# Two iterations of a feed-forward loop brought to the 512-column matmul form of the other eight, on one core

## What is computed

```python
x = x + 0.5 * swiglu(rms_norm(x, ffn1_norm), ffn1_wg, ffn1_wu, ffn1_wd)

def swiglu(x, wg, wu, wd):
    return (silu(x @ wg) * (x @ wu)) @ wd      # wg, wu: 1024 x 2816, wd: 2816 x 1024
```

## Time and profile before

| what | value |
|---|---|
| median of three runs | 859.6 us |
| the profiled execution, its own time | 859.85 us |
| its span, first to last instruction | 858.0 us |
| TensorE busy | 850.4 us (99%) |
| VectorE busy | 640.9 us (75%) |
| ScalarE busy | 526.1 us (61%) |
| granted TensorE clock, mean | 1.000 |
| 24 to 32 us: DMA share | 1.06 |

### The profile page before, as it was taken

How to read it: one execution, slowest core, us unless ns; L and a number is a source line. 1 busy time by engine, 2 the same in 40 slices (tenths; PEclk the granted TensorE clock), 3 DMA queues, 4 the chain that set the end, 5 groups by cost and what they waited for, 6 DMA issues and landing times.

```text
span 858.0 us, 12036 instructions
## 1 busy us (share of the span) xinstructions
PE 850.4 (99%) x4791; PEld 739.4 (86%) x4791; DVE 640.9 (75%) x797; ACT 526.1 (61%) x740; POOL 61.3 (7%) x68
## 2 busy tenths in 40 slices
PE   9999999999999999999999999999999999999997
PEld 8988888888889888888888888888888898888885
DVE  5999999987698756764565468759777777767773
ACT  6777777766574544653553457548766665576762
POOL 0022322210000000000000000100000001000001
PEclk9999999999999999999999999999999999999999
DMA  8976566554644655576456545686656655853501
GB/s 272 325 263 197 179 195 197 196 157 160 200 147 147 198 196 173 175 241 220 149 184 229 176 153 191 215 268 216 227 178 217 216 168 172 260 180 104 180 1 50
DMA packets 124039, 162.47 MB, mean 189 GB/s; under 512 B 3912, under 2 KB 110928, under 8 KB 123984
## 3 DMA queue, kind: packets, MB, share of 16 engines
q1 hardware_dynamic: 122176, 154.89, 55.0%
q0 software_dynamic: 1504, 6.29, 2.3%
q10 hardware_dynamic: 304, 0.53, 0.2%
HBM read 160.65 MB, written 1.05 MB: 188 GB/s over the span
## 4 chain that ended last, share of the span: by engine, by line
PE 99%; POOL 0%; DVE 0%; issue 0%; POOLq 0%
PE pAcc L452 24%; PE pG L396 9%; PE pU L396 9%; PE pAcc L396 7%; PE pG L399 5%; PE pR L396 5%; PE pU L399 5%; PE pM L396 4%; PE pAcc L399 3%; PE pR L399 2%; PE pAcc L430 2%; PE pAcc L432 2%; PE pAcc L431 2%; PE pM L399 2%; PE pG L515 1%; PE pM L430 1%
## 5 line engine op out<-in xcount | busy, mean ns | idle before, releaser
L330 DVE TENSOR_TENSOR lo<-raw,hi 128x2048 fp32r<-128x2048 f32 x131 | 298.4, 2288 | 52.3 <-ACT hi L325 52.3
L325 ACT ACTIVATE hi<-raw 128x2048 fp32r<-128x2048 f32 x140 | 265.6, 1907 | 18.2 <-PE pAcc L432 5.8
L396 PE MATMUL pG<-xT,hi 128*128 128x512 f32 x336 | 83.7, 391 | 0.0
L396 PE MATMUL pU<-xT,hi 128*128 128x512 f32 x320 | 80.2, 392 | 0.0
L452 PE MATMUL pAcc<-hi,h_hi 128*128 128x512 f32 x240 | 74.8, 393 | 0.0
L452 PE MATMUL pAcc<-lo,h_hi 128*128 128x512 f32 x240 | 74.2, 390 | 0.0
L452 PE MATMUL pAcc<-hi,h_lo 128*128 128x512 f32 x240 | 74.0, 389 | 0.0
L396 PEld LDWEIGHTS pG<-xT,hi 128*128 128x128 f32 x336 | 62.1, 188 | 13.0 <-issue 0.7
L1141 ACT ACTIVATE h_hi<-h 128x512 fp32r<-128x512 f32 x28 | 17.7, 633 | 81.0 <-PE pAcc L452 75.2
L396 PEld LDWEIGHTS pU<-xT,hi 128*128 128x128 f32 x320 | 57.5, 189 | 10.3
L1666 DVE TENSOR_TENSOR h_lo<-h,h_hi 128x512 fp32r<-128x512 f32 x28 | 19.2, 688 | 46.1 <-ACT h_hi L1141 46.1
(11 more groups left out here) (520 smaller groups left out, 1650.2 us busy)
## 6 DMA issues: line engine op xcount, KB each, us to landing
raw<-in_a_w_in SPq DMA_DIRECT2D x24, 1024.0 KB, 5.3
raw<-in_ffn_wd SPq DMA_DIRECT2D x22, 1024.0 KB, 5.6
raw<-in_ffn_wg SPq DMA_DIRECT2D x21, 1024.0 KB, 5.4
raw<-in_ffn_wu SPq DMA_DIRECT2D x21, 1024.0 KB, 6.5
raw<-in_w_in SPq DMA_DIRECT2D x16, 1024.0 KB, 5.5
raw<-in_a_w_out SPq DMA_DIRECT2D x8, 1024.0 KB, 4.9
raw<-in_w_kv SPq DMA_DIRECT2D x8, 1024.0 KB, 5.4
raw<-in_b_w_qz SPq DMA_DIRECT2D x8, 1024.0 KB, 5.4
```

The source lines that it names most:

```text
L325: act.activation(HI[n % NHL][:, :], RAW[n % NRAW][:, :], ACT.Copy).then_inc(S["hi"], 1)
L330: dve.tensor_tensor(LO[n % NHL][:, :], RAW[n % NRAW][:, :], HI[n % NHL][:, :].bitcast(f32), ALU.subtract).then_inc(S["lo"], 1)
L396: pe.matmul(v3(bank[:, :], 2), wh[:, k, w], x4[:, :, k, :], start=(k == 0), stop=False, skip_group_check=True)
```

## The change

Iterations 1 and 10 take the 512-column form too. Gate 1 goes to banks R and ACC[0] (`GATE_1`), up 1 and up 10 to G and U. The order on ScalarE and VectorE is rewritten: in iteration 1 `bias_prepare` moves behind the lo part of block 5, and H and both bias sums follow behind it; in iteration 10 `bias_out` comes behind the copies of up 10. TensorE gets a wait for the second sum of the gate in front of each contraction. The rest of the removed lines are the old branches of the same functions.

```diff
-WIDE1 = range(2, 10)
-WIDE = [("ffn1", k, i) for i in WIDE1 for k in ("gate", "up")] + [("ffn1", "gate", NF - 1)]
+WIDE1 = range(1, 10)
+WIDE = [("ffn1", k, i) for i in WIDE1 for k in ("gate", "up")] + [("ffn1", k, NF - 1) for k in ("gate", "up")]
...
         def wide_iteration(pe, i):
             gate, up = ("ffn1", "gate", i), ("ffn1", "up", i)
+            if i == 1:
+                wide_to_features(pe, gate, GATE_1, [(S["xt_lo"], 4)] * 2)
+                pe.wait_ge(S["h_first"], 1)
+                pe.wait_ge(S["h"], 1)
+                for r in range(2):
+                    for t in range(NT):
+                        end = pe.transpose(M[:, r * TOK + t * P:r * TOK + (t + 1) * P],
+                                           H[:, t * BC + r * P:t * BC + (r + 1) * P], IDENT[:, :])
+                end.then_inc(S["hT"], 1)
+                free = [(S["silu"], 1), (S["h"], 1)]
             else:
+                wide_to_features(pe, gate, (G, U), [summed(("ffn1", "up", i - 1), f) for f in range(2)])
+                free = [summed(gate, f) for f in range(2)]
             pe.wait_ge(S["lo"], NTH[up] + 1)
+            wide_to_features(pe, up, (G, U), free)
+            pe.wait_ge(*summed(gate, 1))
+            if i < NF - 1:
+                contract(pe, "ffn1", i - 1)
+        GATE_1 = (R, ACC[0])
...
         def wide_iteration_act(act, i):
...
-            hi(act, n + LEAD)
+            if i > 1:
+                hi(act, n + LEAD)
             act.wait_ge(S["h"], i)
+            banks = GATE_1 if i == 1 else (G, U)
+            wide_act(act, gate, banks, SA, 0)
+            if i > 1:
+                bias_sign(act, step_at(i, 0))
+            wide_act(act, gate, banks, SA, 1)
+            if i == 1:
+                h_hi(act, "ffn1", 0)
+                hi(act, n + LEAD)
             hi(act, n + 1 + LEAD)
             act.wait_ge(*summed(gate, 1))
             act.activation(SA[:, :], SA[:, :], ACT.Silu).then_inc(S["silu"], 1)
             wide_act(act, up, (G, U), SB, 0)
-            bias_sign(act, step_at(i, 1))
+            if i > 1:
+                bias_sign(act, step_at(i, 1))
             wide_act(act, up, (G, U), SB, 1)
+            if i == 1:
+                bias_sign(act, step_at(i, 0))
+                bias_sign(act, step_at(i, 1))
+            if i < NF - 1:
+                hi(act, n + 2 + LEAD)
+                bias_sign(act, step_at(i, 2))
+                bias_sign(act, step_at(i, 3))
+                h_hi(act, "ffn1", i)
...
         def act_ffn(act, ph):
...
+            for i in range(1, NF):
+                wide_iteration_act(act, i)
+            bias_out(act)
+            h_hi(act, ph, NF - 1)
...
         def wide_iteration_dve(dve, i):
...
+            if i == 1:
+                wide_dve(dve, gate, GATE_1, SA, 0)
+                wide_dve(dve, gate, GATE_1, SA, 1)
+                h_lo(dve, "ffn1", 0)
+                lo(dve, n + LEAD)
+                bias_prepare(dve)
+                wide_dve(dve, up, (G, U), SB, 0)
+                wide_dve(dve, up, (G, U), SB, 1)
+            else:
...
             dve.wait_ge(S["hl"], i)
             dve.wait_ge(S["silu"], i + 1)
             dve.wait_ge(*summed(up, 1))
             dve.tensor_tensor(H[:, :], SB[:, :], SA[:, :], ALU.mult).then_inc(S["h"], 1)
-            lo(dve, n + 2 + LEAD)
-            bias_sum(dve, step_at(i, 2))
-            bias_sum(dve, step_at(i, 3))
+            if i == 1:
+                lo(dve, n + 1 + LEAD)
+                bias_sum(dve, step_at(i, 0))
+                bias_sum(dve, step_at(i, 1))
+            if i < NF - 1:
+                lo(dve, n + 2 + LEAD)
+                bias_sum(dve, step_at(i, 2))
+                bias_sum(dve, step_at(i, 3))
             h_lo(dve, "ffn1", i)
```

More of the change, by code:

```diff
@@ L120 @@
     "xt_hi": "their hi parts", "xt_lo": "their lo parts", "out_done": "output stored",
-    "silu": "first gate (bank G) -> SA", "silu_first": "token tile 0 of the very first one", "h_first": "and of its h", "h_half": "first half of the last h of the first layer", "act_b": "second gate (bank U) -> SB", "h": "h in SBUF",
+    "silu": "first gate (bank G) -> SA", "silu_first": "token tile 0 of the very first one", "h_first": "and of its h", "act_b": "second gate (bank U) -> SB", "h": "h in SBUF",
     "wide": "wide blocks half multiplied", "u_half": "last u block half multiplied", "wide_r": "right halves of their banks -> SBUF",
@@ L585, in pe_ffn @@
                 pe.wait_ge(S["lo"], n + 1)
-                if ph == "ffn1" and i in WIDE1:
+                if ph == "ffn1":
                     wide_iteration(pe, i)
@@ L598, in pe_ffn @@
                 else:
[L599 to L606, removed]
-                    else:
-                        wide_to_features(pe, (ph, "gate", i), (G, U), [summed((ph, "gate", i - 1), f) for f in range(2)])
+                    if i == 1:
+                        free = (S["pair_h"], 1), (S["h"], H0[ph] + 1)
+                    else:
+                        free = [summed((ph, "gate", i - 1), f) for f in range(2)]
+                    wide_to_features(pe, (ph, "gate", i), (G, U), free)
                     pe.wait_ge(S["lo"], n + 2)
-                    if ph == "ffn1" and i == NF - 1:
-                        pe.wait_ge(*summed((ph, "gate", i), 0))
-                    elif ph == "ffn1" or i < 3:
+                    if i < 3:
                         pe.wait_ge(S["h"], H0[ph] + i)
                     if i == 1:
-                        if ph == "ffn1":
-                            pe.wait_ge(S["h_first"], 1)
                         for r in range(2):
@@ L621, in pe_ffn @@
                         end.then_inc(S["hT"], 1)
[L622 to L629, removed]
+                    free = ([(S["res"], 8), (S["h"], H0[ph] + 1)] if i == 1 else [(S["h"], H0[ph] + 2)] * 2 if i == 2 else
+                            [summed((ph, "up", i - 1), f) for f in range(2)])
+                    wide_to_features(pe, (ph, "up", i), up_banks(i), free)
                 if ph == "ffn2" and i == 1:
@@ new lines, in dve_ffn @@
+            n = NTH[ph, "gate", 0]
+            if ph == "ffn2":
+                dve.wait_ge(S["hl"], H0[ph])
+                dve.wait_ge(S["pair_silu"], 1)
+                dve.tensor_tensor(H[:, 0:BC], G[:, BC:512], SA[:, 0:BC], ALU.mult).then_inc(S["pair_h"], 1)
+                dve.wait_ge(S["silu"], H0[ph] + 1)
+                dve.tensor_tensor(H[:, BC:512], U[:, BC:512], SA[:, BC:512], ALU.mult).then_inc(S["h"], 1)
+                lo(dve, n + 1 + LEAD)
+                return
+            lo(dve, LEAD)
@@ new lines, in dve_ffn @@
+            dve.wait_ge(S["used"], 2)
+            dve.wait_ge(S["silu"], 1)
+            k = RS_COL["norm", 0, 0][0]
+            dve.wait_ge(S["silu_first"], 1)
+            dve.scalar_tensor_tensor(out=H[:, 0:BC], in0=U[:, 0:BC], scalar=ST[:, k:k + 1], in1=SA[:, 0:BC],
+                                     op0=ALU.mult, op1=ALU.mult).then_inc(S["h_first"], 1)
+            dve.tensor_tensor(H[:, BC:512], U[:, BC:512], SA[:, BC:512], ALU.mult).then_inc(S["h"], 1)
+            lo(dve, 1 + LEAD)
@@ L1969, in m_softmax_dve @@
+            for i in range(1, NF):
+                wide_iteration_dve(dve, i)
         def m_softmax_dve(dve, j):
```

148 lines of the change are left out of this document (25 added, 123 removed).

## The result

The changed kernel takes 864.93 us (median of 6, 863.42 to 866.45) against 859.69 (median of 6, 859.34 to 862.26): the ratio is 1.0055, 95% interval 1.0044 to 1.0065. It is slower by 4.7 us by that ratio; the medians lie 5.2 us apart. Forecast were 861.8 us and a range up to 863.4. The profiled execution took 863.42 us, with a span of 861.6 us; its granted clock over the span is 0.996, and before it was 1.000.

The account below looks back on a forecast made before the run. The prediction took TensorE, busy 99% of the span, as the bound. Iteration 1's +1.74 us and iteration 10's +0.42 made +2.2: 861.8 us against 859.6, with a range of 859.5 to 863.4.

Parts of the forecast that it names:

- What TensorE saves: The 512-column form in iterations 1 and 10 gives back 0.37 us ahead of gate 2 and 0.17 at up 10.
- What iteration 1 adds on VectorE: Sums 1.36 us, later H 0.20 and idle 0.78 move the left sum of gate 2 from 43.45 to 45.79.
- Where that meets TensorE: Ahead of up 2 TensorE waits 2.1 us for bank G, once; net of iteration 1 +1.74 us.
- Iteration 10: The last H comes later than its cover of matmuls; TensorE waits 0.6 us, net +0.42 us.
- The clock: Full clock throughout: 4 us of idle TensorE at the kernel's end kept 1.00, against a 2.1 us wait here.
- rival 4: The wait ahead of up 2 lowers the clock for about one block, costing 5.6 us: 867.4 us; chance 3%.
- rival 3: VectorE's backlog repeats at gate 3 or up 2's second half, about 1 us more: 862.8, both 863.8; chance 10%.
- The sum against the median: Whole kernel: +1.74 and +0.42 make +2.2 us, given as 861.8 us against a median of 859.6.

Follow-up runs that it names:

- undo1: The changed kernel with iteration 1 put back to its old form, iteration 10 left as changed: 860.70 us, ratio 1.0007 to the kernel before.
- after: The changed kernel itself, against the kernel before: median 864.93 us, ratio 1.0055; its profiled execution took 863.42 us.
- undo10: The changed kernel with iteration 10 put back to its old form, iteration 1 left as changed: 862.88 us, ratio 1.0031.
- early: The changed kernel with both sums of gate 2 taken ahead of lo of block 7 and iteration 1's h_lo on VectorE: 863.75 us, ratio 1.0039.
- early_halves: As `early`, with iteration 10's bias_out ahead of the copies of up 10 and the last H made in two halves: 863.76 us, ratio 1.0042.
- after_again: The changed kernel, same code, run again beside `filler_again` on one chip: 863.80 us, ratio 1.0042; its profiled execution took 862.72 us.
- filler_again: Same code as `filler`, run again beside the changed kernel on one chip: 862.65 us, ratio 1.0032 to the kernel before.
- filler: The changed kernel with 18 multiplications by zeros on TensorE between gate 2 and up 2: 863.03 us, ratio 1.0036.
- steps_undo10: The changed kernel with one bias step moved from iteration 1 to iteration 7 and iteration 10 in its old form: 860.43 us, ratio 1.0006.
- alt_undo10: Changed iteration 1, old iteration 10, one bias step moved out of iteration 1, never two four-step iterations in a row: 860.06 us, ratio 1.0004.
- steps: The changed kernel with one bias step of VectorE moved from iteration 1 to iteration 7: 861.37 us, ratio 1.0017.
- delay4: As `steps`, plus one useless sum (1.1 us) on VectorE ahead of the left sum of gate 2: 861.82 us, ratio 1.0025.
- after_gate5: The changed kernel with the load of block 5 held back until block 4 has landed: 865.82 us, ratio 1.0070.

## Why the prediction was wrong

- *What TensorE saves*: right. Gate 1 and up 1 give 11.95 - 11.62 = 0.33 us against 0.37; up 10 takes 186.14 - 180.55 = 5.59 us, as worked out.
- *What iteration 1 adds on VectorE*: right. Sums 0.34 us apart, idle time of 0.53 instead of 0.78 us in front of lo of block 5, H another 0.20 us behind its sum. From gate 1 to the left sum of gate 2 are 45.48 - 21.00 = 24.48 us, worked out as 45.79 - 21.53 = 24.26.
- *Where that meets TensorE*: right, 2.2 us in the profile against 2.1; by the starts gate 2 to up 2 takes 2.4 more. There is no wait ahead of up 3: VectorE catches up, as forecast from 15.56 against 16.62 us.
- *Iteration 10*: right, +0.48 against +0.42 us; VectorE's H starts at 187.31 and `h_lo` 1.39 us later, worked out as 184.16 and 185.61, 1.45 us.

```profile
186.75 0.42 DVE L1825 TENSOR_TENSOR stage_b<-pU,stage_b 128x256 f32<-128x256 f32 x1 [0.65 <-ACT stage_b L1179]
187.31 0.69 DVE L1900 TENSOR_TENSOR h<-stage_b,stage_a 128x512 f32<-128x512 f32 x1
188.70 0.69 DVE L1648 TENSOR_TENSOR h_lo_last<-h,h_hi_last 128x512 fp32r<-128x512 f32 x1 [0.70 <-ACT h_hi_last L1137]
```

- *The clock*: this step failed. It took from the earlier trace rows that 4 us of nothing leave the clock at 1.00, and so put the fall at 3%, tied to a longer wait. The earlier trace rows shows one execution at one place, the end of the kernel, and of the 18 profiles it is the one in which the clock held longest there. The last matmul ends at 851.98 and the fall begins at 857.2, 5.3 us later. In the other 17 the fall at the same place comes 2.0 to 5.0 us behind the last matmul, in nine of them under 3 us. `undo1`, whose last matmul ends at 852.00:

```profile
852.00:854.00 2.00, 0.00 (x0) 0.00 (x0) 0.88 (x4) 1.08 (x5) 1.18 (x2) 1.00 0.00 0
854.00:856.00 2.00, 0.00 (x0) 0.00 (x0) 0.75 (x1) 0.72 (x1) 0.05 (x1) 0.72 0.14 55
```

The changed kernel's 2.23 us were enough in `after`, and 2.2 us in `undo10`, `early` and `early_halves`; 2.24 us were not enough in `after_again`. In 10 of 12 executions of the changed kernel the mean clock is below 0.998. The Trainium skill was cited against the rows with kernels whose pauses between groups of matmuls swing the clock ("TensorE: Matmul & The Clock Gate", Part 1: The HAM clock gate). The trace of the changed kernel agrees in so far as one pause brought one fall, 0.50 at 46 to 49 us; it shows no swinging to and fro. The size in rival 4 was off too: 5.6 us were priced, 1.5 were paid, since the clock came back inside up 2. Rival 4 also needed rival 3's second wait with it; the fall came without one.

- *The sum against the median*: it was made on one profile in which block 4 landed early. Without the fall the change costs 176.20 - 173.49 = 2.7 us where the sum had 2.2 (0.3 of the difference is ahead of up 2), and 859.85 + 2.7 = 862.6 is what `after_again` took (862.72). The fall adds 1.5: about 864.1. So without the fall the time is inside the forecast range, with it outside. The medians are 864.93 and 863.80. A late block 4, for which VectorE no longer has reserve, makes gate 2 to up 2 longer by 1.4 us in the same code (`filler_again` against `filler`), and by 1.2 and 1.0 in `steps_undo10` and `alt_undo10` (6.98 and 6.81 us against the 5.79 of `steps`). Rival 3 named a late block and set it aside because block 9 is asked for earlier; the late one is block 4. That a late block 4 explains the times of 866.0 to 866.5 us is argued, since none of these was profiled, and that it makes the fall likelier is not shown: the two came together in one profile (`delay4`).

## What to carry over

An engine with 75% over the span can have no reserve at all in one stretch; before giving it work, add up its instructions against the bound engine from buffer to buffer. Changing the order of a backlog moves the wait; less work before that point removes it there, and the work may bring a smaller one where it goes (0.4 us in `steps`). A new wait on TensorE is to be priced twice, as its length and as the clock behind it, and a single idle stretch elsewhere at full clock does not show that the clock holds: look at the same stretch in several executions.

## What the hardware showed unexpectedly

Waits of TensorE and the granted clock behind them: 0.5 us (`undo1`), 1.3 (`steps_undo10`) and 1.7 (`filler_again`) at 1.00; 2.2 us at 0.50 in `after`, `undo10`, `early` and `early_halves` and at 1.00 in `after_again`; 2.5 (`delay4`) and 3.7 us (`after_gate5`) at 0.50. This list is one execution each and no limit: `steps`, whose profile has no wait over 0.5 us behind the start, has a mean clock of 0.996 and 0.997 in two executions. In the changed kernel the fall comes at about the end of the wait: the mean is still 0.97 over 45 to 46 us, and TensorE starts at 46.04; in `early_halves` it comes when TensorE has been at work again for a microsecond. And the same transfer of 1 MB, block 4, took 4.9 to 5.8 us in 14 profiles and 6.9 to 7.5 in four, with two more transfers asked for behind it in all four.
